# Spread by transpositions, a 16-column stationary for beta and decay, and a last output tile in two token halves

## What is computed

```
def rms_norm(x, gain):
    y = xf * lax.rsqrt(jnp.mean(xf * xf, axis=-1, keepdims=True) + EPS)
    return (y * gain).astype(x.dtype)

h = x + 0.5 * gate1(c) * SwiGLU_1(adaLN_1(RMSNorm(x), c))
u = adaLN_2(RMSNorm(h), c)
... b_dn, a_dn ... = split(u @ W_in)            # 4 + 4 columns of 7 k
beta = sigmoid(b_dn)
g = -exp(a_log) * softplus(a_dn + dt_bias)
g = cumsum(g) within a block                    # gated delta rule
decay = where(incl, exp(g[:, None] - g[None, :]), 0)
h = h + gate2(c) * mixer(u)
out = h + 0.5 * gate3(c) * SwiGLU_2(adaLN_3(RMSNorm(h), c))
```

## Time and profile before

| | us |
|---|---|
| median of 3 runs | 1262.29 |
| lowest and highest | 1261.52, 1262.78 |
| the profiled execution, its own time | 1262.23 |
| its span, first to last instruction | 1260.5 |
| PE busy in the span | 1235.7 |
| PE weight loads busy | 1004.0 |
| DVE busy | 692.5 |
| ACT busy | 624.7 |

### The profile page before, as it was taken

How to read it: one execution, slowest core, us unless ns; L and a number is a source line. 1 busy time by engine, 2 the same in 40 slices (tenths; PEclk the granted TensorE clock), 3 DMA queues, 4 the chain that set the end, 5 groups by cost and what they waited for, 6 DMA issues and landing times.

```text
span 1260.5 us, 18290 instructions
## 1 busy us (share of the span) xinstructions
PE 1235.7 (98%) x6661; PEld 1004.0 (80%) x6661; DVE 692.5 (55%) x998; ACT 624.7 (50%) x1142; POOL 62.2 (5%) x96
## 2 busy tenths in 40 slices
PE   6999999999999999999999999999999999999998
PEld 5778888888888688787778888877788888888887
DVE  3566666665665784787583655566733333332221
ACT  5477677676554665666863344444422222231221
POOL 0000000001110000000311110002000000000000
PEclk8999999999999999999999999999999999999999
DMA  9666565685553233122231203643233333343330
GB/s 335 186 200 199 175 185 176 197 232 159 159 152 101 66 101 84 51 67 67 52 90 54 76 28 100 200 143 100 68 100 100 100 100 90 93 132 100 110 85 25
DMA packets 278039, 152.41 MB, mean 121 GB/s; under 512 B 8005, under 2 KB 273374, under 8 KB 277982
## 3 DMA queue, kind: packets, MB, share of 16 engines
q1 hardware_dynamic: 273758, 149.54, 40.7%
q10 hardware_dynamic: 4224, 2.10, 0.6%
HBM read 145.31 MB, written 6.29 MB: 120 GB/s over the span
## 4 chain that ended last, share of the span: by engine, by line
PE 90%; DVE 4%; ACT 4%; issue 1%; DMA 1%; SPq 1%; ACTq 0%; DVEq 0%
PE tail L1645 13%; PE tail L1647 13%; PE tail L1646 13%; PE region L1645 13%; PE region L1646 13%; PE region L1647 13%; PE region L1906 1%; PE region L2062 1%; PE region L1814 1%; DVE u_lo L1188 1%; DVE w_lo L1066 1%; ACT w_hi L598 1%; PE region L2066 1%; PE region L1889 1%; PE region L1940 1%
## 5 line engine op out<-in xcount | busy, mean ns | idle before, releaser
L598 ACT ACTIVATE w_hi<-raw 128x1024 fp32r<-128x1024 f32 (+1 forms) x177 | 197.3, 1115 | 422.3 <-PE region L1647 214.4
L1066 DVE TENSOR_TENSOR w_lo<-raw,w_hi 128x1024 fp32r<-128x1024 f32 (+1 forms) x177 | 229.5, 1296 | 214.3 <-ACT w_hi L598 213.5
L1645 PE MATMUL region<-u_hi,w_hi 128*128 128x512 f32 x672 | 262.7, 391 | 1.7 <-DVE u_lo L1188 0.8
L1646 PE MATMUL region<-u_lo,w_hi 128*128 128x512 f32 x672 | 261.7, 389 | 0.0
L1647 PE MATMUL region<-u_hi,w_lo 128*128 128x512 f32 x672 | 261.7, 389 | 0.0
L1645 PEld LDWEIGHTS region<-u_hi,w_hi 128*128 128x128 f32 x672 | 126.1, 188 | 31.0 <-DVE u_lo L1188 2.0
L1645 PE MATMUL tail<-u_hi,w_hi 128*128 128x512 f32 x360 | 146.5, 407 | 2.8 <-DVE w_lo L1066 1.3
L1647 PEld LDWEIGHTS region<-u_hi,w_lo 128*128 128x128 f32 x672 | 126.1, 188 | 26.3
L1646 PEld LDWEIGHTS region<-u_lo,w_hi 128*128 128x128 f32 x672 | 126.1, 188 | 26.0
L1647 PE MATMUL tail<-u_hi,w_lo 128*128 128x512 f32 x360 | 140.5, 390 | 0.0
L1646 PE MATMUL tail<-u_lo,w_hi 128*128 128x512 f32 x360 | 140.3, 390 | 0.0
(11 more groups left out here) (340 smaller groups left out, 1478.3 us busy)
## 6 DMA issues: line engine op xcount, KB each, us to landing
raw<-in_w_ffn_in SPq DMA_DIRECT2D x168, 256.0 KB, 3.4
ada_raw<-in_w_ada SPq DMA_DIRECT2D x56, 512.0 KB, 4.5
raw<-in_w_in SPq DMA_DIRECT2D x90, 256.0 KB, 3.4
raw<-in_w_ffn_out SPq DMA_DIRECT2D x32, 384.0 KB, 5.0
raw<-in_w_ffn_out SPq DMA_DIRECT2D x32, 320.0 KB, 4.1
ada_early<-in_w_ada SPq DMA_DIRECT2D x8, 1024.0 KB, 8.5
gates<-kept_gates SPq DMA_DIRECT2D x16, 256.0 KB, 4.2
raw<-in_w_out SPq DMA_DIRECT2D x16, 256.0 KB, 3.1
```

What stands on the lines that cost most here:

```text
L598: act.activation(w_hi[:, slot % 2, 0:k, :], raw[:, slot, 0:k, :], ACT.Copy).then_inc(hi_ready, 1)
L1066: dve.tensor_tensor(w_lo[:, slot % 2, 0:k, :], raw[:, slot, 0:k, :], w_hi[:, slot % 2, 0:k, :].bitcast(f32), ALU.subtract).then_inc(lo_rea ...
L1645: pe.matmul(bank(b), wh, xh, start=start and n == 0, stop=False)
L1646: pe.matmul(bank(b), wh, xl, start=False, stop=False)
```

## The change

Four things are changed, and nothing else.

1. The root (three places) and the sums of `g` (four blocks) are spread by `pe.transpose` where a matmul stood. For the sums the source is now the column `gsum`, which already holds them, where it was `g` with a triangle.
2. The beta and decay unit has one stationary of 16 columns: the 8 of `w_hi` and, beside them in the same tile, the 8 of the rest, which DVE now writes there. PE runs 16 matmuls with 16 stationary columns, where 24 with 128 stood.
3. `ab_T` has 16 rows. The four transpositions become four float32 matmuls with a new constant `pick` (16 x 8), which adds the two groups of rows while it turns them. DVE makes `pick` once, at the start.
4. The last output tile is computed as two halves of 256 tokens, in banks 7 and 2, with both units' weights for each half. The transpositions of the tile before it stand between the halves. Residual, transpositions, copy and DMA of the last tile are two pieces each.

```diff
-                    ab_T = att_a[0:2 * DNH, 1, 0:S]
+                    ab_T = att_a[0:4 * DNH, 1, 0:S]
...
-            store(KD - 1, 1, KD // 2 - 1)
+            for half in range(2):
+                act.wait_ge(out_ps, KD + half)
+                if half == 0:
+                    act.wait_ge(out_done[1], 16 * (KD // 2 - 1))
+                act.activation(out_nat[:, 1, 2 * half:2 * half + 2],
+                               bank((1, 3)[half])[:, 0:S // 2].rearrange("p (b n) -> p b n", b=2), ACT.Copy)\
+                    .then_inc(out_ready, 1)
+                act.wait_ge(out_ready, KD + half)
+                act.dma_start(out_nat_cols[:, 2 * half:2 * half + 2, (KD - 1) * P:KD * P],
+                              out_nat[:, 1, 2 * half:2 * half + 2]).then_inc(out_done[1], 16)
...
+                if is_static(n) and n == DN_IN:
+                    dve.tensor_tensor(w_hi[:, slot % 2, 0:k, 2 * DNH:4 * DNH], raw[:, slot, 0:k, 0:2 * DNH],
+                                      w_hi[:, slot % 2, 0:k, 0:2 * DNH].bitcast(f32), ALU.subtract).then_inc(lo_ready, 1)
+                    return
...
+                        if f and is_static(i) and i == KD // 2 - 1 and oo == 1:
+                            dve.wait_ge(out_ps, o - 1)
+                            for half in range(2):
+                                cols = slice(half * S // 2, (half + 1) * S // 2)
+                                dve.wait_ge(unit_done, phase + 2 * o + 1 + half)
+                                dve.scalar_tensor_tensor(work[:, 1, cols], bank((7, 2)[half])[:, 0:S // 2],
+                                                         gate_col[:, s, o:o + 1], hT[:, o, cols], ALU.mult, ALU.add)\
+                                    .then_inc(h_ready, 1)
+                            continue
...
+            dve.wait_ge(masks, 10)
+            dve.tensor_tensor(pick[:, :], ident[0:4 * DNH, 0:2 * DNH], ident[0:4 * DNH, 2 * DNH:4 * DNH], ALU.add)
...
                 for b in range(NB):
-                    ins = pe.matmul(bank(4)[:, b * P:(b + 1) * P], tok["rstd"][:, b:b + 1].to_broadcast([P, P]),
-                                    ident[:, :], start=True, stop=True)
+                    ins = pe.transpose(bank(4)[:, b * P:(b + 1) * P], tok["rstd"][:, b:b + 1].to_broadcast([P, P]),
+                                       ident[:, :])
...
+            def narrow():
+
+                pe.wait_ge(proj_ready, 12 - 1)
+                pe.wait_ge(lo_ready, DN_IN + 1)
+                for k in range(KD):
+                    both = w_hi[:, DN_IN % 2, k, 0:4 * DNH]
+                    pe.matmul(bank(6)[0:4 * DNH, :], both, u_hi[:, k, :], start=k == 0, stop=False)
+                    ins = pe.matmul(bank(6)[0:4 * DNH, :], both, u_lo[:, k, :], start=False, stop=k == KD - 1)
+                ins.then_inc(unit_done, 1)
+
-            mixed(0)
+            narrow()
...
-                ins = pe.transpose(bank(3)[:, 8 * b:8 * b + 8], ab_T[:, b * P:(b + 1) * P], ident[0:8, 0:8])
+                ins = pe.matmul(bank(3)[:, 8 * b:8 * b + 8], ab_T[:, b * P:(b + 1) * P], pick[:, :],
+                                start=True, stop=True)
...
-                        ins = pe.matmul(region[e][:, h * P:(h + 1) * P],
-                                        small["g"][:, b, h:h + 1].to_broadcast([P, P]), upto[:, :],
-                                        start=True, stop=True)
+                        ins = pe.transpose(region[e][:, h * P:(h + 1) * P],
+                                           small["gsum"][:, b, h:h + 1].to_broadcast([P, P]), ident[:, :])
...
+            def final_halves(n, between, i):
+
+                pe.wait_ge(lo_ready, n + 2)
+                for half in range(2):
+                    dst, cols = bank((7, 2)[half])[:, 0:S // 2], slice(half * S // 2, (half + 1) * S // 2)
+                    for u in range(2):
+                        slot = (n + u) % 2
+                        for k in range(HALF):
+                            wh, wl = w_hi[:, slot, k, :], w_lo[:, slot, k, :]
+                            xh, xl = g_hi[:, u * HALF + k, cols], g_lo[:, u * HALF + k, cols]
+                            pe.matmul(dst, wh, xh, start=u == 0 and k == 0, stop=False)
+                            pe.matmul(dst, wh, xl, start=False, stop=False)
+                            ins = pe.matmul(dst, wl, xh, start=False, stop=u == 1 and k == HALF - 1)
+                    ins.then_inc(unit_done, 1)
+                    if half == 0:
+                        between(i, 1)
+                for half in range(2):
+                    pe.wait_ge(h_ready, 4 * KD + half)
+                    if half == 0:
+                        pe.wait_ge(out_ready, KD - 2)
+                    for q in range(2):
+                        ins = pe.transpose(bank((1, 3)[half])[:, q * P:(q + 1) * P],
+                                           work[:, 1, (2 * half + q) * P:(2 * half + q + 1) * P], ident[:, :])
+                    ins.then_inc(out_ps, 1)
```

More of the change, by code:

```diff
@@ L160, in build @@
         upto = sb("upto", [P, P])
+        pick = sb("pick", [4 * DNH, 2 * DNH])
         vec = sb("vec", [P, 96])
@@ L826, in mixed @@
                 if kind == "ba":
-                    act.activation(ab_T[:, :], b[0:2 * DNH, :], ACT.Copy).then_inc(proj_ready, 1)
+                    act.activation(ab_T[:, :], b[0:4 * DNH, :], ACT.Copy).then_inc(proj_ready, 1)
                 elif kind == "conv":
@@ L1050, in _ @@
                         store(o - 1, 1 - oo, i - 1 + oo)
-            store(KD - 1, 1, KD // 2 - 1)
+            for half in range(2):
[8 more added lines that the diff above has]
+                              out_nat[:, 1, 2 * half:2 * half + 2]).then_inc(out_done[1], 16)
             act.wait_ge(out_done[0], 16 * KD // 2)
-            act.wait_ge(out_done[1], 16 * KD // 2)
+            act.wait_ge(out_done[1], 16 * (KD // 2 + 1))
         @block.vector
@@ L1743, in ffn_out @@
                         first = is_static(o) and o == 0
+                        if f and is_static(i) and i == KD // 2 - 1 and oo == 1:
+                            final_halves(phase + 2 * o, after, i)
+                            continue
                         if first:
@@ L1774, in _ @@
             for b in range(NB):
-                ins = pe.matmul(bank(4)[:, b * P:(b + 1) * P], tok["rstd"][:, b:b + 1].to_broadcast([P, P]), ident[:, :],
-                                start=True, stop=True)
+                ins = pe.transpose(bank(4)[:, b * P:(b + 1) * P], tok["rstd"][:, b:b + 1].to_broadcast([P, P]),
+                                   ident[:, :])
             ins.then_inc(tok_ps, 1)
@@ L2166, in _ @@
             ffn_out(2, 1, F2_OUT, transpose_last)
-            transpose_out(KD - 1, 1)
 _INS = ["x", "c", "w_ada", "b_ada", "g_ffn1", "w_ffn1_in", "w_ffn1_out", "g_mix", "w_in", "g_q_sb", "g_k_sb", "w_conv",
```

## The result

The changed kernel takes 1268.91 us (median of 5 runs, 1267.91 to 1270.16) against 1262.29 us for the kernel before in the same comparison (1261.52 to 1262.84). The ratio is 1.0054, with a 95% interval from 1.0044 to 1.0065. So it is slower by 6.6 us, beyond the 0.2% that can be told from no change, and 3.3 us above the top of the range that was forecast. The profiled execution took 1268.91 us, with a span of 1267.2 us.

What follows compares the result with a forecast made beforehand. PE was taken to set the time nearly everywhere, busy 1235.7 of 1260.5 us. Terms -1.3 - 0.9 - 0.9 + 3.1 = 0.0 gave 1262.3 us, plus 1.5 for the clock, 1263.8; range 1261.2 to 1265.6.

Steps and rivals of the forecast that it cites:

- unit of 16 matmuls: Beta and decay unit: 24 matmuls become 16 at the same 0.227 us each, all on the path; -1.81 us.
- turn by `pick`: Turn of `ab_T`: four float32 matmuls take 0.95 us where four transpositions took 0.41; +0.54 us on the path.
- spreads, s = 1 and 2: Root spreads: four transpositions take about 0.36 us where 8 instructions took 0.81; 0.45 us gained each, -0.9 us together.
- sums, first pair: Sums of `g`, first pair of blocks: PE's 0.9 us saving only lengthens its wait at L2036; no gain.
- sums, second pair: Sums of `g`, second pair of blocks: DVE idles for them and the chain to L2036 comes earlier; -0.9 us.
- last tile: wait: Front of the last tile: PE waits idle for the second unit's `w_lo`, with nothing to hide it; +3.0 us.
- last tile and clock together: Last tile +3.1 us from wait, narrower matmuls, transpositions and shorter tail; plus 1.5 us for a fall to half clock.
- place of the tensors behind `pick`: No term for moved tensors; only making `pick` on DVE at the start was costed, at nothing, 0.2 us at most.
- the likeliest case: Last tile: the wait comes and PE's clock falls in it, 1262.3 + 1.5 = 1263.8 us; chance 0.50.
- The loads did not pace the halves: Rival for the last tile: weight loads at 0.19 us pace the 256-column matmuls, +9.2 us, 1271.5 us; chance 0.06.
- figure of about 275 ns for a transposition: Rival: read as pace, four transpositions cost 0.29 us more than the 8 instructions replaced, in four places; 1265.3 us; chance 0.02.
- The chance of 0.19 for slower: Whole kernel above 1264.8 us: paced loads 0.06, the page's transposition rule 0.02, longer low clock or too kind sum 0.11.

Runs made afterwards that it cites:

- unshifted: The changed kernel with `pick` put into unused bytes, so every large tensor lies where it did before; all four edits stand; 1263.73 us, ratio 1.0011.
- pad32: The kernel before with an unused tensor of 32 bytes per partition where `pick` stands, and nothing else; 1267.28 us, ratio 1.0040.
- filled: `unshifted` with 12 more matmuls of 512 columns, results unread, at the front of the last tile where PE would be idle; 1261.74 us, ratio 0.9996.
- placed: `woven` with unused bytes giving `g`, `m`, `ysb`, `ydn` the weights' remainder and starting early load targets at multiples of 512; 1255.80 us, ratio 0.9950.
- woven: `unshifted` with the last tile run unit by unit: first unit for both halves, earlier tile's transpositions, second unit for both halves; 1259.11 us, ratio 0.9975.
- pad192: The kernel before with 192 unused bytes where `pick` stands, moving `g` and `m` to the weights' remainder; 1259.74 us, ratio 0.9980.
- gap_in_front: The kernel before with 64 unused bytes ahead of `hT`, moving `u`, weights, `g` and `m` together; 1262.57 us, ratio 1.0003.

## Why the prediction was wrong

The terms of the sum, one by one, first as predicted, then as the traces and runs have them:

| term | predicted, us | measured, us |
|---|---|---|
| unit of 16 matmuls | -1.8 | -1.7 (231 ns each, not 227) |
| turn by `pick` | +0.5 | +0.6 |
| spreads, s = 1 and 2 | -0.9 | -0.85 (trace) |
| sums, first pair | 0 | 0, the wait at L2074 grew by 0.97 |
| sums, second pair | -0.9 | -0.85 (trace) |
| last tile: wait | +3.0 | +2.84 idle, +3.1 in the account |
| last tile and clock together | +3.1 + 1.5 | +3.9 (runs), +4.4 (traces) |
| place of the tensors behind `pick` | 0, 0.2 at most | +5.2 (against `unshifted`), +4.9 (`pad32`) |

**The step that failed** is the one sentence on `pick`: "`pick` is made by DVE before the first tokens are there; I cost it at nothing for the same reason, 0.2 us at most." It costs the making of `pick`: `unshifted`, which makes `pick` too, takes what the sum has, so nothing speaks against that. It doesn't ask what allocating it does. 32 bytes ahead of `g_hi`, `g_lo`, `m_hi` and `m_lo` changed their distance to the weights from -192 to -160 bytes and the time from start to start from about 229 to 233.3 ns, in some 1,180 matmuls of 512 columns that the change doesn't touch: 990 on `g` x 3.7 + 192 on `m` x 4.3 ns = 4.5 us, of the 5.2 that separate the changed kernel from `unshifted`. Behind it stands an assumption that the text never named: that an unchanged instruction keeps its duration. With the 4.9 us of `pad32` in that step's place, the sum is 1263.8 + 4.9 = 1268.7, against 1268.91 measured.

**What held.** The wait at the front of the last tile was read from the earlier trace rows within 0.2 us, and its place is where the text had it. The clock fell because of it, as the likeliest case said, though 0.4 us behind its end and not in it. The price taken, 1.5 us, agrees with the traces (1.5) and less with the runs of `filled` (2.0), but by luck: it was the middle between no fall and 6.8 us at half clock, and what came was 3.4 us. The pace of 256 columns is 0.120 us. The text had worked out "at least 0.12" and then took 0.118, against its own bound; over 132 matmuls that is 0.3 us. The gain of the first pair was lost at the next wait, as argued from the earlier trace rows. That the kernel without the displacement takes 1263.73 us, 0.1 from the forecast, is partly luck: by the medians the end came out 0.7 us cheaper than forecast and the transpositions gained 0.8 less, and the two cancel. By the traces both are within 0.2 us.

**The rivals.** The loads did not pace the halves (0.120 us, where that case needed 0.19). The Trainium skill's figure of about 275 ns for a transposition in "TensorE: Matmul & The Clock Gate" (Part 4, PE-mode transpose), read as a pace, was wrong here: four transpositions take 0.36 us from their start to the next matmul's. The chance of 0.19 for slower held none of what happened. It was made of three mechanisms in the edited code, and the cause was in code that was not edited.

**What the Trainium skill has on it.** The traces show that the pace of a matmul of 512 columns changes with the distance of its two operands in the partition, by some 6 ns of 227. The Trainium skill, in "TensorE: Matmul & The Clock Gate" (Step-by-step: what each phase is for), says that TensorE reads the moving operand and the weights through two independent ports, and that loading the next weights takes no read bandwidth from the running matmul. If nothing but that counted, the distance would not matter, and the change would have taken 1263.8 us. The measurements disagree with that reading, and they decide. Whether it is the two reads that disturb each other, no trace here shows: the profile has only the starts, and the work is the same.

## What to carry to other kernels

Before costing an edit, ask what it moves that it doesn't touch: a new tensor of 32 bytes in the middle of the allocation was here worth more than all of the edits together (5.2 us against 1.4, the sum of their gains and costs). Put new small tensors behind everything or into free bytes, and compare the pace of the unchanged groups first when a trace comes back. Where a kernel is bound by long rows of matmuls with a new stationary for each, try the distance between the moving and the stationary operand as a parameter of its own: here equal remainders by 512 bytes gained 3.3 us for a few hundred unused bytes of each partition (`placed` against `woven`, 1255.80 against 1259.11). Measure it for each width: at 256 columns the same remainder was 2 to 6 ns slower.

## What the runs showed of the hardware that I had not expected

- **Pace and place.** 227, 229.6 or 233.3 ns from start to start on average for the same matmul of 512 columns, by the distance in bytes between its operands. The period and the rule are not settled: distances of 32, 64, 96, 128, 160 and 224 bytes below were slow, 192 half so, and 0 fastest, but for `ysb` in `pad192` (228.6) and the matmuls of 256 columns.
- **Loads and place.** The loads into `ada_early` (1 MB) and `ada_raw` (512 KB) took longer to land where the tensors behind `pick` were moved, by 32 to 192 bytes. Issues after (KB, us to landing), then the same in `unshifted`:

```profile
ada_raw<-in_w_ada SPq DMA_DIRECT2D x56, 512.0 KB, 5.1
...
ada_early<-in_w_ada SPq DMA_DIRECT2D x8, 1024.0 KB, 9.6
```

```profile
ada_raw<-in_w_ada SPq DMA_DIRECT2D x56, 512.0 KB, 4.5
...
ada_early<-in_w_ada SPq DMA_DIRECT2D x8, 1024.0 KB, 8.4
```

  In `placed` they are at 4.5 and 8.6 again; in `gap_in_front`, with all moved by 64 bytes, `ada_raw` is at 4.5 and `ada_early` at 9.2, so the place of the target alone doesn't explain both. What does stays open. What it cost isn't shown: the second group on `ada_early` starts at 16.55 in the changed kernel, and between 15.91 and 16.63 in the kernels in which nothing is displaced.
- **A short idle time lowers the clock in the midst of dense work.** 2.84 us without a matmul, between stretches in which PE was busy throughout, and the granted clock stood at half for 3.4 us, from 0.4 us (changed kernel) or 1.1 us (`unshifted`) after PE had started again; with the same stretch filled by useless matmuls it stayed full.
